# V rows gathered as 32 tokens of four experts each, multiplied by 128x32 stacks of diagonals in four column groups

## The chip, the cores and the metric

One of the cores of a Trainium2 chip runs the whole kernel. The metric is device time in microseconds, from the first to the last instruction of an execution; the median of several executions counts.

## The reference

A decoder layer on 512 tokens of width 1024: gated mixers, a cross-attention, and then a channel mixer with 16384 single-neuron experts, of which each token picks 128 (8 heads, the best 16 of each). Only the last part is touched:

```python
def chunk_fn(args):
    xb, ib, gb = args                  # 128 tokens, their expert numbers (128 each), their gates
    u = expert_u[ib]                   # (128, 128, 1024) rows of the U table
    act = jax.nn.gelu(jnp.einsum('ced,cd->ce', u, xb))
    return jnp.einsum('ce,ced->cd', gb * act, expert_v[ib])
out = lax.map(chunk_fn, (xc, ic, gc))
```

So each token needs 128 dot products with its own U rows and then the weighted sum of 128 V rows of its own. All is float32; both tables are 64 MB.

## The kernel before, in words

**Steps and slots.** The tokens are four tiles of 128. Tile and head make 32 groups of 16 steps; a step (512 in all, called tau or a slot) is one expert of each of the 128 tokens of a tile. In step n GpSimd gathers 128 rows of U, one per token (`u_rows`, eight places, L576; 512 KB), and VectorE forms the 128 dot products (`dot`, L1391). When a group of 16 is through, `gelu` on VectorE and ScalarE turns dots and gates into weights in eight parts over the next eight slots. `select` on VectorE picks the experts of a group, two pieces per slot, about two groups ahead. Steps 0 to 255 are tiles 0 and 1 (h = 0) and run under the front layers of tiles 2 and 3; steps 256 to 511 are tiles 2 and 3 (h = 1). Slots below are counted from step 256 (`HSTEPS`). Every engine walks the slots in the same order and does what lists give for each; they wait for each other only through data and places.

**V for tiles 0 and 1, densely.** From one-hot vectors of the two halves of each expert's number the kernel makes the whole matrix of weights, tokens by experts, and multiplies it with the whole V table. 64 chunks: `one_hots` on VectorE (every third of the first 32 partly on ScalarE, `first_hots`), `gate_chunk` on TensorE (L886), `take_gates` on ScalarE. 128 blocks: the SP queue brings 512 KB of V each in four places (`d_rows`), `dense_block` multiplies (L896). Chunks 0 to 31, blocks 0 to 63, chunks 32 to 63, blocks 64 to 127, by `CH_SLOT` and `BLK_SLOT`.

**V for tiles 2 and 3, by gathers.** V row m (0 to 255) is expert e = m mod 16 of group 16 + m div 16, for 128 tokens. GpSimd gathers it (L590) in `v_rows`, 6 places at first and 8 from the second chunks on, and at the end also in `u_rows`; a place is free when the pair of its last row is multiplied (`wait_used`, `v_used`). V_SLOT says at which slot row m is multiplied; the gather stands `V_AHEAD` = 4 slots later in GpSimd's order, which itself may be 8 slots ahead of the dots. A gather that waits for its place holds up all gathers behind it, U rows too. ScalarE makes a diagonal matrix of the row's 128 weights (`diagonal`, L1091): two diagonals of 64x64, one below the other, in eight places (`DRING`), two slots ahead, four slots behind in the last slots. `expert_pair(m)` on TensorE multiplies rows m and m + 1: odd rows are gathered with the token halves exchanged (`idx_turned`, made at L1384; their weights are exchanged at L1436), so that with two rows each of the four 64x64 tiles of the array has a result of its own: row half r and result half o, eight matmuls of 64x64 by 64x512 for a pair, in four banks. `add_experts(i)` on VectorE (L1468) adds both pairs of banks to tile 2 + i, the first at the slot after row 127 and the second at the end. TensorE waits for the first before row 128, as both tiles use the same banks.

**The end.** After the last rows: `add_experts(1)`, the norm of ScalarE (`finish_norm`), the scaling (`finish`, L1482), the store by the SP queue (L537).

**How a matmul shows in the trace.** A float32 matmul is two records, each with its weight load. A pair of V rows is 16 records, a dense block 8, a chunk 16.

## Time and profile before

| | us |
|---|---|
| median of 3 runs | 2024.65 (2023.76 to 2026.74) |
| span of the profiled execution | 2043.0 |
| TensorE busy | 1942.4 (95%) |
| VectorE busy | 1190.6 (58%) |
| GpSimd busy | 870.7 (43%) |
| ScalarE busy | 445.9 (22%) |
| DMA | 613.48 MB, mean 300 GB/s |

The profile is of one execution on the slowest (here the only) core, with times from its first instruction. PE is TensorE, PEld its weight loads, DVE VectorE, ACT ScalarE, POOL GpSimd, SP the sync engine; SPq is a queue of transfers. A line such as L846 is a line of the kernel. In the rows below a name such as `ps<-v_rows,diag` is result and operands, x16 a count; in a timeline, what stands in brackets is the idle time before and what ended it. "DMA share" is how busy the 16 DMA engines were together, over 1 where their packets overlap. Some matmul records can be missing from a trace.

### The profile page before, as it was taken

The page shows a single profiled execution, that of the slowest core. Times are in us where ns is not written, and L with a number is a line of the kernel's source. Part 1 is how long each engine was busy: PE and PEld are TensorE (multiplying, and loading weights), DVE is VectorE, ACT ScalarE, POOL GpSimd, SP SyncE. Part 2 cuts the span into 40 slices and gives each one's busy share as a digit, 9 for nine tenths or more (in the row PEclk, how much of TensorE's full clock was granted, in tenths as well). Part 3 has the DMA queues.
Part 4 walks back from the last instruction along what each step waited for, and adds up shares of the span by engine and source line. Part 5 has one row for each costly group of instructions (what it writes and reads, how often), then busy time and mean ns, then how long its engine had stood idle before and what let it go on. Part 6 is the DMA issues. An engine that isn't in the chain of part 4 may idle for free.

```text
span 2043.0 us, 23964 instructions
## 1 busy us (share of the span) xinstructions
PE 1942.4 (95%) x9007; PEld 1255.0 (61%) x9007; DVE 1190.6 (58%) x2972; ACT 445.9 (22%) x1045; POOL 870.7 (43%) x785
## 2 busy tenths in 40 slices
PE   8999999999889999999998888999999989999998
PEld 7688886956775887885676765444445543333332
DVE  1022101003896888788899989887867775444321
ACT  2233211111202454121211354000013321101112
POOL 0000000000684423445658355844557776666543
PEclk9999999999999999999999568999999999999999
DMA  7543454434999877999899677999999999999997
GB/s 237 147 121 109 148 155 144 145 103 136 373 388 349 280 255 239 369 386 388 331 359 371 221 261 243 410 409 409 409 376 348 344 334 410 409 409 409 409 389 278
DMA packets 252439, 613.48 MB, mean 300 GB/s; under 512 B 18676, under 2 KB 121124, under 8 KB 252324
## 3 DMA queue, kind: packets, MB, share of 16 engines
q0 software_dynamic: 110592, 402.70, 52.5%
q1 hardware_dynamic: 141120, 208.17, 29.7%
q8 instruction: 72, 1.18, 0.2%
q10 hardware_dynamic: 612, 1.07, 0.2%
q14 instruction: 43, 0.35, 0.0%
HBM read 609.77 MB, written 2.10 MB: 300 GB/s over the span
## 4 chain that ended last, share of the span: by engine, by line
PE 65%; DMA 13%; DVE 9%; POOL 7%; issue 3%; another core or an unknown queue 1%; ACT 1%; SPq 0%; POOLq 0%; DVEq 0%; ACTq 0%
PE ps L617 26%; PE ps L896 11%; PE ps L846 8%; DMA u_rows<-in_peer_u_dram,idx 7%; PE ps L632 7%; POOL u_rows L576 5%; DVE u_rows L1391 4%; PE ps L886 3%; PE ps L659 3%; POOL v_rows L590 2%; DMA wring<-in_w_in_dram 2%; DMA v_rows<-in_peer_v_dram,idx_turned 2%; PE ps L646 1%; PE ps L685 1%
## 5 line engine op out<-in xcount | busy, mean ns | idle before, releaser
L576 POOL DMA_INDIRECT u_rows<-in_peer_u_dram,idx x512 | 584.5, 1142 | 977.1 <-DVE idx L1378 508.2
L1391 DVE CUSTOM_DVE_ANT_0 u_rows<-u_rows,xn 128x1024 f32<-128x1024 f32 x512 | 621.3, 1217 | 177.8 <-DMA u_rows<-in_peer_u_dram,idx 165.2
L617 PE MATMUL ps<-xT,wring 128*128 128x256 f32 x2432 | 553.1, 386 | 22.3 <-DMA wring<-in_w_in_dram 10.1
L617 PEld LDWEIGHTS ps<-xT,wring 128*128 128x128 f32 x2432 | 464.0, 193 | 90.8 <-DMA wring<-in_w_in_dram 11.0
L896 PE MATMUL ps<-d_rows,gates 128*128 128x512 f32 x1024 | 456.3, 600 | 0.8 <-issue 0.8
L896 PEld LDWEIGHTS ps<-d_rows,gates 128*128 128x128 f32 x1024 | 190.7, 191 | 266.6 <-issue 266.6
L846 PE MATMUL ps<-v_rows,diag 64*64 64x512 f32 x1928 | 256.9, 633 | 18.9 <-DMA v_rows<-in_peer_v_dram,idx_turned 16.4
L590 POOL DMA_INDIRECT v_rows<-in_peer_v_dram,idx x121 | 135.4, 1119 | 131.3 <-PE ps L846 98.6
L886 PEld LDWEIGHTS ps<-hot_b,hot_a 128*128 128x128 f32 x1024 | 147.2, 230 | 55.4 <-issue 36.0
L886 PE MATMUL ps<-hot_b,hot_a 128*128 128x64 f32 x1024 | 155.0, 318 | 19.3 <-DVE hot_b L1458 11.0
L1091 ACT ACTIVATE diag<-ident,wgt 128x64 f32<-128x64 f32 x256 | 75.8, 336 | 435.6 <-PE ps L846 351.5
L846 PEld LDWEIGHTS ps<-v_rows,diag 64*64 64x64 f32 x1928 | 71.3, 138 | 162.1 <-issue 149.0
L590 POOL DMA_INDIRECT v_rows<-in_peer_v_dram,idx_turned x120 | 133.3, 1111 | 36.6 <-issue 34.7
L1450 DVE TENSOR_TENSOR hot_a<-e1T,iota_a 128x1024 f32<-128x1024 f32 x54 | 65.6, 1214 | 39.6 <-remote 27.1
L1123 ACT ACTIVATE gates<-ps 128x512 f32<-128x512 f32 x64 | 66.7, 1062 | 70.4 <-PE ps L886 67.5
L1231 DVE SCALAR_TENSOR_TENSOR spb_a<-ps,spb_a 128x384 f32<-128x384 f32 (+1 forms) x16 | 13.2, 824 | 85.6 <-ACT spb_a L1018 85.0
L1250 DVE TENSOR_TENSOR merged<-ps,sgc 128x256 f32<-128x256 f32 x16 | 6.7, 421 | 91.5 <-PE ps L617 91.5
L617 PE MATMUL ps<-qT,wring 128*128 128x256 f32 x256 | 56.8, 380 | 1.4 <-DMA wring<-in_w_branch_attn_dram 1.4
L617 PE MATMUL ps<-yconv,wring 128*128 128x256 f32 x256 | 56.8, 380 | 0.9 <-DMA wring<-in_w_branch_conv_dram 0.9
L632 PE MATMUL ps<-wring,xT 128*128 128x512 f32 x128 | 55.6, 592 | 0.0
L617 PEld LDWEIGHTS ps<-qT,wring 128*128 128x128 f32 x256 | 48.7, 190 | 8.3 <-DMA wring<-in_w_branch_attn_dram 1.8
L617 PEld LDWEIGHTS ps<-yconv,wring 128*128 128x128 f32 x256 | 48.7, 191 | 7.7 <-DMA wring<-in_w_branch_conv_dram 1.3
(201 smaller groups left out, 1747.0 us busy)
## 6 DMA issues: line engine op xcount, KB each, us to landing
wring<-in_w_in_dram SPq DMA_DIRECT2D x128, 512.0 KB
d_rows<-in_peer_v_dram SPq DMA_DIRECT2D x128, 512.0 KB
wring<-in_peer_w_query_dram SPq DMA_DIRECT2D x32, 512.0 KB
wring<-in_w_branch_conv_dram SPq DMA_DIRECT2D x16, 512.0 KB
wring<-in_w_branch_attn_dram SPq DMA_DIRECT2D x16, 512.0 KB
wring<-in_w_out_dram SPq DMA_DIRECT2D x16, 512.0 KB
wring<-in_xattn_wq_dram SPq DMA_DIRECT2D x16, 512.0 KB
wring<-in_xattn_wo_dram SPq DMA_DIRECT2D x16, 512.0 KB
```

The source lines that it names most:

```text
L576: pool.indirect_dma_start(out=u_rows[:, n % URING, :], out_offset=None, in_=peer_u[0], in_offset=bass.IndirectOffsetOnAxis(ap=experts_of(g ...
L590: pool.indirect_dma_start(out=v_row(m), out_offset=None, in_=peer_v[0], in_offset=bass.IndirectOffsetOnAxis(ap=own, axis=0)).then_inc((v_r ...
L617: mm = pe.matmul(bank(job)[:, 0:HN], w[:, k % 4, P * b:P * (b + 1)], act[:, k, :], start=(k == 0), stop=(k == KT - 1))
L632: mm = pe.matmul(bank(job + i), act[:, k, P * i:P * (i + 1)], w[:, k % 2, :], start=(k == 0), stop=(k == KT - 1))
L659: mm = pe.matmul(bank(job + i), act[:, k, P * i:P * (i + 1)], w[:, k % 2, :], start=(k == 0), stop=(k == KT - 1))
L846: mm = pe.matmul(ps[o:o + 64, 2 * (r // 64) + c, :], diag[r:r + 64, k % DRING, :], v_row(k)[r:r + 64, BANK * c:BANK * (c + 1)], start=firs ...
L886: mm = pe.matmul(ps[:, 4 + ch % 4, 64 * t:64 * (t + 1)], hot_a[:, 8 * (ch % 2) + t, :], hot_b[:, ch % 2, t, :], start=True, stop=True)
L896: mm = pe.matmul(ps[:, 4 + 2 * i + c, :], gates[:, j % 64, P * i:P * (i + 1)], d_rows[:, j % 4, BANK * c:BANK * (c + 1)], start=(j % 64 == ...
L1091: act.activation(diag[:, m % DRING, :], ident64[:, :], ACT.Copy, scale=wgt[:, g, e:e + 1]).then_inc(diag_rdy, 1)
L1123: act.activation(gates[:, :, t:t + 8].rearrange("p b t -> p t b"), ps[:, 4 + ch % 4, :].rearrange("p (t b) -> p t b", t=8), ACT.Copy).then ...
L1391: dve.tensor_tensor_reduce(out=u, in0=u, in1=(xn2 if h else xn1)[:, i, :], scale=1.0, scalar=0.0, op0=ALU.mult, op1=ALU.add, accum_out=dot ...
L1450: dve.tensor_tensor(hot_a[:, 8 * (ch % 2):8 * (ch % 2) + 8, :], e1T[:, i, o:o + 8].unsqueeze(2).to_broadcast([P, 8, P]), iota_a[:, :].unsq ...
```

## The change

Row m = 16 g + 4 s + b now holds, for token block b of 32 tokens, four experts: partition 32 q + j is the V row of token 32 b + j for its expert 4 q + s. With a stack of four 32x32 diagonals as the stationary (128x32) one matmul sums over the four experts and gives 32 tokens. Rows m to m + 3 (b = 0 to 3) make up the 128 tokens, in the four column groups of the array.

- `expert_quad(m)` for `expert_pair(m)`: 8 matmuls of 128x32 by 128x512 for four rows, in place of 8 of 64x64 by 64x512 for two. Each token tile has two banks of its own, so `add_experts` is one addition per tile and the wait for `hadd` goes. Places of V rows are freed by fours.
- Indices and weights must be laid out by blocks: 16 small copies per group on VectorE (`idx_quad`, in the last four pieces of `select`) for two, and 16 small copies per group on ScalarE (`spread_weights`) for the exchange in the last part of `gelu`, which is one product now. `gelu` waits in part 4 until the last group's weights are spread.
- `diag` is 128x32 in 12 places for 128x64 in 8. A diagonal is made no earlier than its group's weights (`WEIGHTS_AT`).
- `v_rows` has 6 places, 8 from the slot where GpSimd is past the selection of tile 2, 10 past that of tile 3.
- The lists of slots are new. Chunks begin at slot 16 for 12, blocks at 52 for 48 and at 181 for 179. V rows by slot:

| slots | rows before | slots | rows after |
|---|---|---|---|
| 24 to 46 | 22 | 24 to 46 | 26 |
| 48 to 150 | 14 | 46 to 80 | 25 |
| | | 115 to 150 | 7 |
| 151 to 177 | 84 | 150 to 178 | 104 |
| 179 to 256 | 110 | 178 to 210, 210 to 240, 240 to 256 | 32, 31, 9 |
| 256 to 280 | 26 | 256 to 268, 268 to 280 | 17, 5 |

```diff
-    URING, VRING, DRING, GRING, IRING = 8, 8, 8, 4, 8
+    URING, VRING, DRING, GRING, IRING = 8, 10, 12, 4, 8
+    BLOCK = P // 4
...
-    CH_SLOT = spread(12, 46, 32) + spread(151, 177, 32)
+    CH_SLOT = spread(16, 46, 32) + spread(151, 177, 32)
...
-    BLK_SLOT = spread(48, 149, 64) + spread(179, 260, 64)
-    V_SLOT = (spread(24, 46, 22) + spread(48, 150, 14) + spread(151, 177, 84) + spread(179, 256, 110)
-              + spread(256, 280, 26))
+    BLK_SLOT = spread(52, 149, 64) + spread(181, 260, 64)
+    V_SLOT = (spread(24, 46, 26) + spread(46, 80, 25) + spread(115, 150, 7) + spread(150, 178, 104) + spread(178, 210, 32) + spread(210, 240, 31) + spread(240, 256, 9) + spread(256, 268, 17) + spread(268, 280, 5))
...
+    WEIGHTS_AT = [HSTEPS + TOPK * (g + 1) + 8 for g in range(HG)]
     for m, slot in enumerate(V_SLOT):
         V_OF.setdefault(slot + V_AHEAD, []).append(m)
-        DIAG_OF.setdefault(slot + (DIAG_BEHIND if slot >= STEPS - 16 else -DIAG_AHEAD), []).append(m)
-        if m % 2:
-            PAIR_OF.setdefault(slot, []).append(m - 1)
+        DIAG_OF.setdefault(max(slot + (DIAG_BEHIND if slot >= STEPS - 16 else -DIAG_AHEAD), WEIGHTS_AT[m // TOPK]),
+                           []).append(m)
+        if m % 4 == 3:
+            QUAD_OF.setdefault(slot, []).append(m - 3)
...
-    V_LATE = next(m for m in range(HSTEPS) if V_SLOT[m] >= CH_SLOT[32])
+    V_GROWS = {next(m for m in range(HSTEPS) if V_SLOT[m] + V_AHEAD > TOPK * (HG + PH * (n + 1) - 1)): n
+               for n in range(HT)}
...
         def wait_used(eng, m):
-            eng.wait_ge(v_used, m // 2 + 1)
+            eng.wait_ge(v_used, m // 4 + 1)
...
-                        pool.wait_ge(turned, 2 * (g + 1))
-                    own = idx_turned[:, g, e // 2:e // 2 + 1] if e % 2 else idx2[:, g, e:e + 1]
+                        pool.wait_ge(quad_idx, 16 * (g + 1))
                     pool.indirect_dma_start(
                         out=v_row(m), out_offset=None, in_=peer_v[0],
-                        in_offset=bass.IndirectOffsetOnAxis(ap=own, axis=0)
+                        in_offset=bass.IndirectOffsetOnAxis(ap=idx_quad[:, g, e:e + 1], axis=0)
                     ).then_inc((v_ready if kind == "v" else u_ready)[place], 16)
...
-            def expert_pair(m):
+            def expert_quad(m):
                 if m == 0:
                     pe.wait_ge(wt_done, 2 * SBH)
-                if m == HSTEPS // 2:
-                    pe.wait_ge(hadd, 2)
-                pe.wait_ge(diag_rdy, m + 2)
-                for k in (m, m + 1):
-                    wait_row(pe, k)
-                first, last = m % (HSTEPS // 2) == 0, m % (HSTEPS // 2) == HSTEPS // 2 - 2
+                tile, n = m // (HSTEPS // 2), m % (HSTEPS // 2)
+                pe.wait_ge(diag_rdy, m + 4)
+                for b in range(4):
+                    wait_row(pe, m + b)
                 for c in range(2):
-                    for k, turn in ((m, 0), (m + 1, 64)):
-                        for r in (0, 64):
-                            o = (r + turn) % P
-                            mm = pe.matmul(ps[o:o + 64, 2 * (r // 64) + c, :], diag[r:r + 64, k % DRING, :],
-                                           v_row(k)[r:r + 64, BANK * c:BANK * (c + 1)],
-                                           start=first, stop=last)
+                    for b in range(4):
+                        mm = pe.matmul(ps[BLOCK * b:BLOCK * (b + 1), 2 * tile + c, :], diag[:, (m + b) % DRING, :],
+                                       v_row(m + b)[:, BANK * c:BANK * (c + 1)],
+                                       start=(n == 0), stop=(n == HSTEPS // 2 - 4))
                 mm.then_inc(v_used, 1)
...
+            def spread_weights(g):
+                act.wait_ge(wgt_rdy, HG + g + 1)
+                for b in range(4):
+                    for q in range(4):
+                        to = wgt[BLOCK * q:BLOCK * (q + 1), g, :].rearrange("p (s b) -> p s b", b=4)[:, :, b]
+                        qw = act.activation(to, gl[BLOCK * b:BLOCK * (b + 1), 3, 4 * q:4 * (q + 1)], ACT.Copy)
+                qw.then_inc(quad_wgt, 1)
...
-                    act.wait_ge(v_used, (m - DRING) // 2 + 1)
-                act.activation(diag[:, m % DRING, :], ident64[:, :], ACT.Copy,
+                    act.wait_ge(v_used, (m - DRING) // 4 + 1)
+                act.activation(diag[:, m % DRING, :], ident32[:, :], ACT.Copy,
                                scale=wgt[:, g, e:e + 1]).then_inc(diag_rdy, 1)
...
+                if tau in WEIGHTS_AT:
+                    spread_weights(WEIGHTS_AT.index(tau))
...
-                    odd = idx2[:, g - HG, :].rearrange("p (e two) -> p e two", two=2)[:, :, 1]
-                    for r in (0, 64):
-                        dve.tensor_copy(idx_turned[64 - r:P - r, g - HG, :], odd[r:r + 64, :]).then_inc(turned, 1)
+                    for b in range(4):
+                        for q in range(4):
+                            to = idx_quad[BLOCK * q:BLOCK * (q + 1), g - HG, :].rearrange("p (s b) -> p s b", b=4)
+                            dve.tensor_copy(to[:, :, b], idx2[BLOCK * b:BLOCK * (b + 1), g - HG,
+                                                              4 * q:4 * (q + 1)]).then_inc(quad_idx, 1)
+                        yield
...
                     dve.wait_ge(gate_rdy, g + 1)
+                    if g > HG:
+                        dve.wait_ge(quad_wgt, g - HG)
...
-                for r in range(2):
-                    if r:
-                        dve.wait_ge(hadd, 2 * i + 1)
-                    dve.tensor_tensor(hh, ps[:, 2 * r:2 * r + 2, :].rearrange("p c n -> p (c n)"), hh,
-                                      ALU.add).then_inc(hadd, 1)
+                dve.tensor_tensor(hh, ps[:, 2 * i:2 * i + 2, :].rearrange("p c n -> p (c n)"), hh,
+                                  ALU.add).then_inc(hadd, 1)
```

## Rows read from the trace of the kernel before

**Rows 1.** The page's slices: GB/s of the transfers, 40 slices of 51 us

```profile
GB/s 237 147 121 109 148 155 144 145 103 136 373 388 349 280 255 239 369 386 388 331 359 371 221 261 243 410 409 409 409 376 348 344 334 410 409 409 409 409 389 278
```

**Rows 2.** Windows, all engines: stretch, length, busy time of each, clock, DMA share, GB/s

```profile
1130.00:1268.00 138.00, 120.81 (x689) 95.50 (x690) 128.35 (x272) 70.39 (x151) 63.57 (x59) 0.67 0.71 231
1268.00:1505.00 237.00, 234.32 (x624) 100.25 (x623) 185.99 (x531) 9.44 (x42) 135.54 (x124) 1.00 1.02 405
1505.00:1678.00 173.00, 156.56 (x1201) 87.50 (x1202) 137.36 (x269) 53.12 (x123) 127.09 (x109) 0.96 0.95 343
1678.00:1972.00 294.00, 293.68 (x1236) 107.82 (x1240) 117.66 (x303) 32.13 (x114) 183.29 (x174) 1.00 1.02 407
1972.00:2043.00 71.00, 60.93 (x352) 21.87 (x344) 11.89 (x20) 12.71 (x41) 26.57 (x28) 0.97 0.80 300
```

**Rows 3.** Timeline of TensorE, pieces of E, D and B: start, length, instructions

```profile
1835.65 3.70 PE L896 MATMUL ps<-d_rows,gates 128*128 128x512 f32 x8
1839.29 3.66 PE L846 MATMUL ps<-v_rows,diag 64*64 64x512 f32 x32
1842.88 7.13 PE L896 MATMUL ps<-d_rows,gates 128*128 128x512 f32 x16
...
1518.49 2.00 PE L886 MATMUL ps<-hot_b,hot_a 128*128 128x64 f32 x16
...
1203.55 3.68 PE L886 MATMUL ps<-hot_b,hot_a 128*128 128x64 f32 x16 [1.48 <-DVE hot_b L1458]
1207.16 3.69 PE L846 MATMUL ps<-v_rows,diag 64*64 64x512 f32 x16
```

**Rows 4.** Timeline of TensorE, the column groups of L711 in the first half

```profile
116.32 0.43 PE L711 MATMUL ps<-wbuf_a,vbuf 128*64 128x256 f32 x1
116.33 0.43 PE L711 MATMUL ps<-wbuf_b,vbuf 128*64 128x256 f32 x1
116.59 0.38 PE L711 MATMUL ps<-wbuf_a,vbuf 128*64 128x256 f32 x1
```

**Rows 5.** Groups of instructions by shape, VectorE, stretch B

```profile
L1450 DVE TENSOR_TENSOR hot_a<-e1T,iota_a 128x1024 f32<-128x1024 f32 x22 | 26.6, 1209 | 6.0 <-PE ps L886 4.8 <-issue 1.1
...
L1384 DVE COPY idx_turned<-idx 64x8 uint32<-64x8 uint32 x4 | 0.7, 165 | 0.1
```

**Rows 6.** Timeline, small work of ScalarE and VectorE in B

```profile
1166.24 0.20 ACT L1081 ACTIVATE gl<-gl 128x16 f32<-128x16 f32 x1
...
1174.61 0.35 ACT L1091 ACTIVATE diag<-ident,wgt 128x64 f32<-128x64 f32 x1 [4.26 <-DVE wgt L1436]
...
1173.88 0.70 DVE L1436 SCALAR_TENSOR_TENSOR wgt<-gl,gate_r 128x8 f32<-128x8 f32 x3
```

**Rows 7.** Waits, stretch E: engine and line, waited for, us, times, longest

```profile
DVE u_rows L1391 <- DMA u_rows<-in_peer_u_dram,idx: 121.9, 51, 5.2
...
DVE hbuf L1468 <- issue: 21.0, 1, 21.0
```

**Rows 8.** Timeline of VectorE at the end

```profile
2034.30 2.48 DVE L1468 TENSOR_TENSOR hbuf<-ps,hbuf 128x1024 f32<-128x1024 f32 x2 [8.51 <-PE ps L846]
```

**Rows 9.** Windows of L896 and of L846 alone, stretch F

```profile
1972.00:2043.00 71.00, 28.97 (x64) 11.77 (x64) 0.97 0.80 300
...
1972.00:2043.00 71.00, 32.74 (x288) 10.11 (x280) 0.97 0.80 300
```

**Rows 10.** Chain of work that ended last, one piece in C: start, length, what

```profile
1363.42 17.13 DMA u_rows<-in_peer_u_dram,idx
```

**Rows 11.** Timeline, a gather of D and the pair that uses its row

```profile
1573.71 1.02 POOL L590 DMA_INDIRECT v_rows<-in_peer_v_dram,idx_turned  x1 [0.30 <-issue]
...
1579.93 1.52 PE L846 MATMUL ps<-v_rows,diag 64*64 64x512 f32 x12 [0.47 <-DMA v_rows<-in_peer_v_dram,idx_turned]
```

**Rows 12.** Timeline of GpSimd, stretch F

```profile
1997.45 0.94 POOL L590 DMA_INDIRECT v_rows<-in_peer_v_dram,idx  x1 [0.30 <-issue]
```

**Rows 13.** Waits, stretch F

```profile
POOL v_rows L590 <- PE ps L846: 16.8, 5, 4.2
```

42 lines of the change are left out of this document (21 added, 21 removed).

## The prediction

> **What bounds the kernel now.** I read the page's shares of engines first, then its slices, then the same figures cut at the borders of the work. TensorE is busy 95% of the span, but from slice 24 on slices with 409 GB/s stand beside slices with a quarter to a half less [rows 1]. Both are near a limit, so the question is which of them ends last in each stage. The change touches only what comes after 1130 us, so I cut that part in five [rows 2]:
>
> - B, 1130 to 1268: one-hot chunks 0 to 31, 22 V rows. VectorE busy 128.35 of 138 us, 231 GB/s, TensorE's mean clock 0.67.
> - C, 1268 to 1505: dense blocks 0 to 63, 14 V rows. TensorE 234 of 237 us, 405 GB/s: both full.
> - D, 1505 to 1678: chunks 32 to 63, 84 V rows. TensorE 157 and GpSimd 127 of 173 us, 343 GB/s.
> - E, 1678 to 1972: dense blocks and V rows. TensorE 293.68 of 294 us, 407 GB/s: both full again.
> - F, 1972 to 2043, the end: 300 GB/s.
>
> The most that any slice shows is 409 GB/s, at a DMA share of 1.03. A gather or a block of the V table is 512 KB, so a transfer costs 524288 / 409000 = 1.28 us when the queues are full. No byte is removed by this change: 256 V rows are gathered before and after. A stage can only win what it leaves of 409 GB/s: B 138 x (1 - 231/409) = 60 us, C 2, D 28, E 1, F 19. That is 110 us, and it is the ceiling of any gain here. In E DMA is as full as TensorE, so halving TensorE's work gives nothing unless V rows move out of E, and where they go they cost at least their transfer.
>
> **Part 1, the multiplication.** A pair of V rows is 8 matmuls of a 64x64 stationary, 16 records; in E two pairs take 3.59 us from start to start, 1.80 each [rows 3]. Afterwards four rows are 8 matmuls of 128x32, again 16 records of 512 columns. If four column groups run side by side as the four 64x64 tiles do, a quad also costs 1.80: 64 quads are 115 us in place of 128 pairs, 230. No row shows four groups. The nearest is L711: two 128x64 column groups, each with its own moving tile, start at 116.32 and 116.33, and the next two begin 0.26 later [rows 4]. So two groups take the time of one, with weights of all 128 rows loaded under running matmuls. Bounds for a quad: 1.80 (all four), 3.6 (two at a time), and 16 x 0.455 = 7.3 us (none; 0.455 is a record of L896, 8 in 3.64 us from start to start [rows 3]). I take 1.80, because the nearest row has full overlap. Below 1.80 nothing speaks for: the records stream as many columns.
>
> [...]
>
> **Part 2, the new small work.** VectorE: 16 index copies per group of 16 steps in place of 2, and one weight product in place of three. Copies stand at 165 ns [rows 5] and three products take 0.70 us [rows 6]. 14 x 0.17 - 0.45 = +1.9 us per group. In C and E VectorE waits for U rows (122 us in E [rows 7]) and hides it; in B it is the bound. Four groups (16 to 19) are selected before B ends, so +7.6 us there. ScalarE: 16 tiny copies per group. The shortest ScalarE row is 0.20 us [rows 6]; a diagonal of 64 columns takes 0.35 at most places and is the high bound [rows 6]. So 3.2 to 5.6 us per group, I take 3.5. ScalarE is busy 70 of 138 us in B and 53 of 173 in D [rows 2] and has room, but everything behind it on its queue (the diagonals, the takings of gates) is late by as much once per group. PE waits for that where a quad needs fresh weights; in B that is group 17 at slot 40. It is cheap: 2 us. GpSimd's two additions for the identity come once before B; nothing. One add of experts in place of two: 2.48 us for two [rows 8], so -1.2 us at the end. The first token tile's add also moves on VectorE, from slot 184 to 169, into the chunks of D; it now waits 21 us for TensorE in E [rows 7], where dots are behind it and U rows cover it. In D one-hots are behind it, but TensorE is within a chunk or two of VectorE there, so at most two chunks of 2.00 us and a quad, 6 us; I leave it in D's 9 us of waits, of which TensorE's own share goes away. TensorE's wait for hadd at row 128 goes (the second tile has banks of its own); TensorE is never idle there, so nothing. The wait for quad_wgt ahead of the product in gelu: behind it on VectorE is the next dot. ScalarE passes spread_weights 8 slots after a group's end, the wait comes 20 slots after it. Nothing, while ScalarE is under 12 slots late.
>
> **Part 3, the places.** V rows by stage, from the lists of slots: B 22 to 26, C 14 to 32, D 84 to 104, E and F 136 to 94. A quad can't start before its group's weights, which are ready 8 slots after the group's last dot. From group 10 on the lists put the first quad of a group 2 to 6 slots before that, so TensorE must lag VectorE by about 5 slots in E. Now it lags similarly: 8 blocks (64 records) and 36 V rows (288) are left to it when the dots are through [rows 9].
>
> *B.* It ends at slot 46, not 48: -4 us (two slots of 1.2 us of dot and 0.7 of selection). +7.6 VectorE, +2 ScalarE. 6 quads for 11 pairs, and VectorE's 6 us of idling ahead of its one-hots shrink [rows 5]: -4. Sum about +1; bounds -6 and +10.
>
> *C.* 237 us x 405 GB/s is 183 transfers; +18 V and +2 U of the two slots are 203, x 1.28 = 260 us. TensorE needs 64 x 3.64 + 8 x 1.80 = 247 and is no longer the bound. +23; low bound +12 (TensorE's 247 and 2). High bound: V has six places here, so of a quad's four rows two are issued only after the quad before. Three gathers, a landing as long as the 17 us of a U row [rows 10] and 2 us of quad are 23 us, and slots 46 to 80 want a quad every 16.7 (5.4 slots of 2.4 transfers). Over 6 quads that would be 38 us, but fewer transfers in flight land sooner; a fifth of it stays: +30.
>
> *D.* GpSimd issues every gather: 109 in 127.09 us, 1.17 each, plus 0.30 between two [rows 2, 11], so 1.47 a gather. 28 U + 84 V = 112 x 1.47 = 164, and 9 us of waits make the 173 of now. Afterwards 132 x 1.47 = 194 + 9 = 203. TensorE's 27 x 1.80 + 63 = 112 us are far below. +30. Low end 132 x 1.28 = 169 plus 9 = 178 (+5), if GpSimd's durations fall to the 0.94 that it shows where VectorE is quiet [rows 12]; high end in rival 1.
>
> *E and F.* 294 x 407 + 71 x 300 GB/s are 269 transfers; 42 fewer are 227, x 1.28 = 291 us. TensorE: 64 x 3.64 + 23.5 x 1.80 = 275, below. Behind the last byte come the last quad (2 us) and then add, norm, scaling and store: 9 us from the adds on now, to the span's end at 2043.0 [rows 8]; -1.2, so 10 in all. 301 for 365: -64, of which 54 are the 42 rows and 10 the end, where GpSimd now waits for TensorE (16.8 us in five waits [rows 13]) and the queues stand empty. Bounds -70 and -50.
>
> **Sum.** +1 +23 +30 -64 = -10 us of the profiled span of 2043.0. The three timed runs have a median of 2024.65, 18 us less than the span, so I carry the difference over: 2014.6, -0.5%.
>
> **Rivals.**
>
> 1. *Places freed by quads, and the clock, starve D: slower.* A place is freed only when all four rows are used. From a quad's end, four V rows and a U are issued (4.08 x 1.47 = 6.0 us to the last), it lands 6.2 later (issued 1573.71, used 1579.93 [rows 11]), the quad takes 1.9: 14.1 us for two quads, 7.05 each, under GpSimd's 5.08 x 1.47 = 7.5. But TensorE has work for 112 of 203 us. It was busy 157 of 173 at clock 0.96 now, and 121 of 138 at 0.67 in B [rows 2]; there, at half clock, 16 records take 3.69 us in place of 1.80 and a chunk 3.68 in place of 2.00 [rows 3]. At half clock D needs 27 x 3.69 + 32 x 3.68 = 217 us, so D is bound by it, and the cycle of places becomes (14.1 + 1.8 + half a chunk) / 2 = 8.9 x 26 = 231. D between 217 and 231, +44 to +58, for +30: the sum is +4 to +18, say 2036. It decides once the clock stays at half for more than 203/217 of D. For it: the clock of B. Against it: B's 0.67 is no half (0.50) either; TensorE that has fallen behind is busy and gets its clock back, and in D it would be busy at half clock.
> 2. *Column groups only by twos.* Quad 3.6 us: C 233 + 29 = 262, +25; D 27 x 3.6 + 63 = 160, under its bound, +30; E 233 + 85 + 9 = 327, -38. The sum with B is +18: 2042. None at all: C +54, D 27 x 7.3 + 63 + 9 = 269, +96, E 233 + 172 + 9 = 414, +49: 2225.
> 3. *GpSimd speeds up and D and B gain more.* D +5, B -4, C and E at their middle: -40, 1985. For it: GpSimd's gathers are 1.17 in D and 0.94 in F [rows 12]. Against it: VectorE, beside which they are long, has the same work in D.
> 4. *It is hidden.* The four terms cancel to within 4 us: what E loses is what C and D take, 42 rows at 1.28 there against 38 at 1.28 to 1.47 here. Time 2021 to 2028.
>
> [...]
>
> **How the numbers follow.** Forecast (-4 to -25 us) 0.42; rival 3 (beyond -25) 0.16; rival 4 0.17; rival 1 0.18; rival 2 0.07. A change of 0.2%, 4 us, is about what a measurement of this kernel tells from none. Faster 0.58, same 0.17, slower 0.25. The range takes in rival 3 to its middle, rival 1 whole and rival 2's first case: 1988 to 2043. The likeliest case alone is 2000 to 2021.
>
> **What would show it.** Part 1: a stretch of two quads takes 3.6 us, the matmuls of the four column groups start together, and all of them 115 us busy. C: 405 to 409 GB/s with TensorE idle for 10 us or more, waiting for V rows. D: 200 us or so, GpSimd back to back, TensorE near 60% busy, its clock the thing to look at. E: 300 us to the end, no longer 100% TensorE, VectorE's wait for U rows shorter. End: 409 GB/s to within 20 us of the last byte. I am wrong if a quad takes over 2 us at full clock, if D takes over 215 us, or if the queues are not full in C and E, for then TensorE waits for V rows whose places are not free and blocks and dots wait behind it.

## The result and the profile after

Measured: 2055.91 us, median of 4 runs (2052.8 to 2058.24), against 2025.7 (2023.76 to 2027.34) for the kernel before beside them. The ratio is 1.0139 [1.0116, 1.0162]: slower by 1.4%, 41 us above the forecast of 2014.6 and 13 above the upper end of its range, 2043.

The windows of the changed kernel. Their borders are events, since the lists of slots moved: first one-hot chunk, first dense block, end of the 64th block, the next block, end. I call the five stretches A to E; A is what lies ahead of the prediction's B (here from 1000 us), and E takes in its F. Columns as in [rows 2].

```profile
1000.00:1135.94 135.94, 113.00 (x474) 79.70 (x472) 129.84 (x372) 16.88 (x45) 92.83 (x75) 0.93 0.98 356
1135.94:1288.17 152.23, 122.99 (x640) 99.25 (x640) 138.87 (x319) 79.73 (x201) 81.02 (x70) 0.60 0.69 238
1288.17:1528.40 240.23, 236.08 (x612) 100.40 (x608) 180.41 (x559) 30.51 (x145) 150.36 (x126) 0.98 1.02 405
1528.40:1750.36 221.96, 158.77 (x945) 88.13 (x945) 147.45 (x301) 65.66 (x190) 152.68 (x137) 0.72 0.93 335
1750.36:2051.00 300.64, 273.51 (x884) 107.70 (x880) 129.09 (x345) 44.13 (x191) 166.57 (x155) 0.96 0.99 388
```

Cut by the same events, the profiled execution of before is A 133.1, B 134.7, C 234.5, D 175.5, E 365.2 us. So E is 64.6 us shorter, as forecast, and A to C are 26 longer where 24 were forecast; D is 222 us for 175.5, +46.5 where +30 was forecast. Its clock fell from 0.96 [rows 2] to 0.72. D lies in the 31st to 34th slices, which have 316 to 340 GB/s; before, it had 334 to 348 in the 31st to 33rd [rows 1].

```profile
PEclk9999999999999999999998565999996877999999
...
GB/s 236 151 116 114 147 150 148 139 113 135 382 386 391 275 246 256 384 389 389 329 361 353 215 232 262 386 402 409 409 398 316 337 340 339 393 395 384 407 409 339
```

The quad (four V rows multiplied together) is itself what was hoped for. TensorE in D (start, length, instructions): 16 records of 128x32 in 1.92 us at full clock (granted 1.00 from 1583.40 to 1588.40) and in 3.64 at half clock (0.50 from 1548.40 to 1558.40), and ahead of most quads of D a wait for a V row.

```profile
1558.31 3.64 PE L849 MATMUL ps<-v_rows,diag 128*32 128x512 f32 x16
...
1575.64 3.64 PE L849 MATMUL ps<-v_rows,diag 128*32 128x512 f32 x16 [3.52 <-DMA v_rows<-in_peer_v_dram,idx_quad]
1579.21 4.19 PE L889 MATMUL ps<-hot_b,hot_a 128*128 128x64 f32 x32
1583.33 1.92 PE L849 MATMUL ps<-v_rows,diag 128*32 128x512 f32 x16
1585.19 2.00 PE L889 MATMUL ps<-hot_b,hot_a 128*128 128x64 f32 x16
1589.55 2.94 PE L849 MATMUL ps<-v_rows,diag 128*32 128x512 f32 x16 [2.37 <-DMA v_rows<-in_peer_v_dram,idx_quad]
```

The waits of D, changed kernel (engine and line, what for: us, times, longest):

```profile
DVE hot_a L1463 <- PE ps L889: 60.6, 15, 9.3
PE ps L849 <- DMA v_rows<-in_peer_v_dram,idx_quad: 50.5, 20, 6.8
POOL v_rows L597 <- PE ps L849: 34.4, 13, 14.5
...
POOL v_rows L597 <- issue: 29.2, 91, 1.7
...
PE ps L849 <- ACT diag L1102: 10.2, 1, 10.2
```

TensorE waits for V rows, GpSimd can't issue them because TensorE hasn't given their places back, and VectorE's one-hots and U gathers queue behind both. That is a ring of waits with no engine full: TensorE 159, GpSimd 153, VectorE 147 of 222 us. GpSimd is the nearest to full: with the 0.30 us between two of its 137 gathers it is taken for 194. In D of the kernel before it waited 13.8 us for TensorE (and 8.1 more for something that its trace doesn't name), TensorE 16.4 for V rows.

### The profile page after: what moved, and what is told of

Its sections match the earlier page's. It is cut to its first block, busy times and chain, and to the rows that moved or that the text cites. A ratio compares the mean times of both kernels' runs of the same rounds, so it can differ in the third digit from the quotient of the medians.

```text
span 2051.0 us, 22378 instructions
## 1 busy us (share of the span) xinstructions
PE 1865.9 (91%) x7983; PEld 1234.3 (60%) x7983; DVE 1221.0 (60%) x3162; ACT 488.5 (24%) x1301; POOL 898.6 (44%) x787
## 3 DMA queue, kind: packets, MB, share of 16 engines
q1 hardware_dynamic: 141120, 208.17, 29.6%
## 4 chain that ended last, share of the span: by engine, by line
PE 55%; DMA 16%; POOL 11%; DVE 10%; issue 6%; ACT 2%; POOLq 0%; ACTq 0%; DVEq 0%
PE ps L624 25%; PE ps L899 8%; DMA u_rows<-in_peer_u_dram,idx 7%; PE ps L639 7%; POOL v_rows L597 6%; DVE u_rows L1407 5%; POOL u_rows L584 5%; DMA v_rows<-in_peer_v_dram,idx_quad 5%; PE ps L849 5%; PE ps L889 3%; PE ps L666 2%; DMA wring<-in_w_branch_attn_dram 2%; DMA wring<-in_w_in_dram 1%; PE ps L653 1%; PE ps L692 1%
## 5 line engine op out<-in xcount | busy, mean ns | idle before, releaser
L584 POOL DMA_INDIRECT u_rows<-in_peer_u_dram,idx x512 | 607.5, 1186 | 907.7 <-DVE idx L1391 507.9
L597 POOL DMA_INDIRECT v_rows<-in_peer_v_dram,idx_quad x247 | 276.8, 1121 | 223.2 <-PE ps L849 143.3
L849 PE MATMUL ps<-v_rows,diag 128*32 128x512 f32 x988 | 171.3, 818 | 101.7 <-DMA v_rows<-in_peer_v_dram,idx_quad 69.8
L889 PEld LDWEIGHTS ps<-hot_b,hot_a 128*128 128x128 f32 x1024 | 165.7, 256 | 71.6 <-DVE hot_b L1471 38.7
L889 PE MATMUL ps<-hot_b,hot_a 128*128 128x64 f32 x1024 | 172.5, 344 | 26.4 <-DVE hot_b L1471 24.4
L849 PEld LDWEIGHTS ps<-v_rows,diag 128*32 128x32 f32 x988 | 34.2, 133 | 188.1 <-issue 144.6
L1102 ACT ACTIVATE diag<-ident,wgt 128x32 f32<-128x32 f32 x256 | 62.2, 307 | 157.5 <-PE ps L849 157.1
L1091 ACT ACTIVATE wgt<-gl 32x4 f32<-32x4 f32 x256 | 52.9, 207 | 139.2 <-DVE gl L1451 136.4
```

What stands on the lines that cost most here:

```text
L584: pool.indirect_dma_start(out=u_rows[:, n % URING, :], out_offset=None, in_=peer_u[0], in_offset=bass.IndirectOffsetOnAxis(ap=experts_of(g ...
L597: pool.indirect_dma_start(out=v_row(m), out_offset=None, in_=peer_v[0], in_offset=bass.IndirectOffsetOnAxis(ap=idx_quad[:, g, e:e + 1], ax ...
L849: mm = pe.matmul(ps[BLOCK * b:BLOCK * (b + 1), 2 * tile + c, :], diag[:, (m + b) % DRING, :], v_row(m + b)[:, BANK * c:BANK * (c + 1)], st ...
L889: mm = pe.matmul(ps[:, 4 + ch % 4, 64 * t:64 * (t + 1)], hot_a[:, 8 * (ch % 2) + t, :], hot_b[:, ch % 2, t, :], start=True, stop=True)
L1091: qw = act.activation(to, gl[BLOCK * b:BLOCK * (b + 1), 3, 4 * q:4 * (q + 1)], ACT.Copy)
L1102: act.activation(diag[:, m % DRING, :], ident32[:, :], ACT.Copy, scale=wgt[:, g, e:e + 1]).then_inc(diag_rdy, 1)
```

## The experiments

All ratios below are to the kernel before on the same chip. Even so they compare only within one of two kinds of chips: on two chips (e1 to e8) the kernel before had a median of 2042 us and the changed one a ratio of 1.0076 (e7); on the others (e9 to e18) it had 2026 to 2027, as in the result above with its 1.0139. The changed kernel itself takes the same time on both, 2055.7 and 2055.9 us; the kernel before does not. e2 to e6 and e8 were run on the first kind alone, and the runs that mend the loss (e10, e12, e14, e15, e17, e18) on the second alone, so a step from one group to the other mixes the edit with the kind of chip. To compare stretches I use "left": a stretch's length x (1 - its GB/s / 409), my estimate of the time by which its bytes could have been moved sooner; 409 to 411 GB/s is the most that a slice of any of these profiles shows. Each figure for a stretch is of one profiled execution.

**e1_before, e16_before: the kernel before, one profile each.**

> The kernel before, profiled once more. The profile that the prediction rests on has a span of 2043.0 us beside timed runs of 2024 to 2027; the profiled run of the changed kernel (2051.0) lies 5 us under its own median. If the 18 us were an effect of profiling on this kernel, this span is again near 2043 with the same stages (B 135, C 237, D 173, E with the end 365). If that execution was merely a slow one, this span is 2022 to 2030, and the missing 15 to 20 us stand in one or two places of the stages, which then were mis-sized in the sum.

> The kernel before, unchanged, one profile. Both of its profiles so far leave 27 and 28 us of 409 GB/s in D; e10, e13 and e14 leave 16, e15 leaves 27. If D's loss belongs to the kernel, it is 26 to 28 us again; if it differs from execution to execution, it may be 16 as in e13, which in D has the same form and the same eight places.

2034.93 us on a chip of the first kind (D 174.7 us, 26.9 left), and 2024.75 on one of the second. The latter, windows as above:

```profile
1126.86:1257.38 130.52, 116.89 (x689) 92.06 (x689) 123.31 (x259) 70.41 (x151) 60.72 (x57) 0.69 0.71 233
1257.38:1493.10 235.72, 234.66 (x628) 100.38 (x624) 184.44 (x532) 9.44 (x42) 140.98 (x125) 1.00 1.02 404
1493.10:1659.28 166.18, 146.56 (x1200) 84.53 (x1201) 140.20 (x271) 53.24 (x122) 123.50 (x109) 0.97 0.98 366
1659.28:2022.90 363.62, 354.36 (x1588) 129.57 (x1584) 129.50 (x322) 44.98 (x155) 213.41 (x202) 0.99 0.98 387
```

D takes 166.2 us and leaves 17.5, where the execution on which I built the sum took 175.5 and left 27.9. So what D leaves differs by 10 us between profiles of one kernel. Whether executions or chips differ so isn't settled: e1 is of the first kind and e16 of the second, and the chip of the profile of [rows 2] isn't on record. The execution of [rows 2] was 20 us longer than this one: 9.2 in A to C (6.2 of them in A, which the change hardly touches), 9.3 in D, 1.6 in E. Against e16, the changed kernel costs +35 in A to C, +56 in D and -63 in E.

**e2_quads_old_lists: the changed kernel with the lists of slots of before.**

```
-    CH_SLOT = spread(16, 46, 32) + spread(151, 177, 32)
-    BLK_SLOT = spread(52, 149, 64) + spread(181, 260, 64)
+    CH_SLOT = spread(12, 46, 32) + spread(151, 177, 32)
+    BLK_SLOT = spread(48, 149, 64) + spread(179, 260, 64)
(and V_SLOT)
```

> The changed kernel (quads, stacks of diagonals, 12 diagonals, the new small work) with the three lists of slots of the kernel before. Theory A, the places: the loss comes from moving 42 V rows forward into stages where places are freed by fours and TensorE falls to half clock. Then B takes 5 us more than before for the small work, C as before, D 168 to 178 us (21 quads at 8.0 us, the rate that the changed kernel shows), E with the end 345 to 357: 2010 to 2030. Theory B, the quads themselves: the small work of VectorE and ScalarE and the waits for whole quads cost wherever they stand. Then D is 185 or more, B 150, and the time 2040 to 2060.

1.0043 [1.0015, 1.0071]. Slower without the new lists too: D leaves 36.9 us, for 26.9 in e1 on the same chip. TensorE waits 47.1 us there for V rows (5.5 in e1), GpSimd 29.6 for TensorE (17.0). The end gained: the last 66 us leave 11.8 for 19.8.

**e3_pairs_new_lists: pairs of 64x64 with the new lists.**

```
-            PAIR_OF.setdefault(slot, []).append(m - 1)
+            PAIR_OF.setdefault(V_SLOT[m | 3], []).append(m - 1)
```

> The kernel before (pairs of 64x64) with the new lists of slots; both pairs of four rows stand at the slot of the last row, and a diagonal is made no earlier than its group's weights, as the new lists need. Eight places at the most. Theory A: D is bound by places and a low clock; pairs keep TensorE busier (54 pairs are 97 us for 49) and free places a little sooner, so D is 195 to 210 for 217, E TensorE-bound at 327 to 340 for 301; 2055 to 2080. Theory B: without the quads' small work B falls back to 137 and D to 190, and the whole is below 2045.

1.0121 [1.0054, 1.0188]. Both pairs of four rows stand at the slot of the fourth. The end leaves 26.5 us: pairs can't keep up there. D leaves most of all, 48.7, although a pair frees its places by itself. It holds two things together, the new lists and pairs put off to the fourth row's slot; no run has pairs at their own slots with the new lists.

**e4_filler: the changed kernel with two unused matmuls per one-hot chunk, ahead of the wait for it.**

```
+                for _ in range(2):
+                    pe.matmul(ps[:, 4 + ch % 4, :], ident[:, :], xn2[:, 0, 0:BANK], start=True, stop=True)
                 pe.wait_ge(hot_rdy, ch + 1)
```

> The changed kernel with two matmuls of 128x128 by 128x512 (four records, 1.8 us at full clock) ahead of each chunk's wait for its one-hots, in the chunk's own bank, which the chunk then overwrites. If the half clock is what costs in B and D, the mean clock rises to 0.9 or more, a chunk takes 2.0 and a quad 1.9 us for 3.6, and D falls from 217 to about 200, B by 5 us: 2030 to 2040. If places and landings bound D whatever the clock, the clock rises and D stays at 210 to 220, and the time is 2050 to 2065; if the filler itself gets in the way, TensorE has 58 us more in each of B and D and the time rises over 2065.

1.0076 [1.0044, 1.0107], the same as the changed kernel on the other chip of that kind (e7). Its window of D:

```profile
1528.60:1755.59 226.99, 185.09 (x1073) 99.06 (x1073) 148.52 (x306) 66.18 (x190) 149.21 (x137) 0.88 0.91 328
```

The granted clock rose from 0.72 to 0.88 in D and from 0.60 to 0.92 in B (151.6 us), and neither got shorter. The unused matmuls take time themselves (TensorE is busy 185 us in D for 159, 135 in B for 123), so this run alone doesn't say that the clock is free. e6 and e17 say more: they have the same halves, clocks of 0.91 and 0.95 in D, and D takes 219.7 us in one and 195.2 in the other.

**e5_pairs_by_fours: the kernel before, only that who waits for a free place waits for four rows at a time.**

```
-            eng.wait_ge(v_used, m // 2 + 1)
+            eng.wait_ge(v_used, 2 * (m // 4) + 2)
```

> The kernel before with one edit: a place of a V row is free only when all four rows of its four are multiplied (the pairs, the lists and the rest stay). Theory A, places freed by fours cost: in D GpSimd waits longer for TensorE, TensorE longer for V rows, and what D leaves of 409 GB/s rises from 27 us to 33 to 38, the whole is 5 to 12 us slower than before, nearly all of the +7 us that quads with the old lists show in D. Theory B, it is the quad's own matmuls or waits: the same time as before to within 3 us.

1.0031 [1.0009, 1.0053]. D leaves 36.5 us where e1 leaves 26.9, and GpSimd waits 28.9 us for TensorE where it waited 17.0. So releasing by fours costs 0.3% by itself, without a quad. That D then leaves what it leaves in e2 rests on one profile of each, and e16 shows that such a figure can differ by 10 us in one kernel.

**e6_halves: the changed kernel, rows 0 to 159 multiplied and freed by twos, both halves at the quad's slot.**

```
+                for part in ((0, 1), (2, 3)) if m < HALVED else ((0, 1, 2, 3),):
+                  pe.wait_ge(diag_rdy, m + part[-1] + 1)
```

> The changed kernel, but rows 0 to 159 are multiplied and freed by twos (two column groups at a time, TensorE waits for two rows, not four); from row 160 on quads as they are. Theory A, places: D's transfers leave 30 to 34 us of 409 GB/s in place of 40, D falls from 222 to 212 to 216, B by 0 to 5, TensorE's mean clock in D rises over 0.85 as its work there doubles: 6 to 15 us under the changed kernel. Theory B, D is bound by GpSimd's issuing and by the late weights alone: no change, within 4 us of the changed kernel. It also tells the price of two column groups: 3.6 us for four rows if only two run at a time.

1.0074 [1.0044, 1.0103] for e7's 1.0076: nothing, where theory A wanted 6 to 15 us. D's clock was 0.91 and its length 219.7, and GpSimd waited 30.0 us for TensorE in it, TensorE 32.2 for V rows. The first half is still asked for only when the fourth row is due, so by my estimate its places come back about the length of a half ahead of the second's (1.91 us for 8 records, at 1600.80).

**e7_after: the changed kernel again, on e6's chip.**

> The changed kernel again, beside the kernel before on this chip, as the partner for the others of this call: 1.2 to 1.6% slower than before, with the stages that it showed (B 152, C 240, D 222, E 301).

1.0076 [1.0049, 1.0103], where 1.012 to 1.016 were expected; D 229.5 us, 44.9 left, clock 0.69.

**e8_indices_by_act: e2 with the 16 index copies on ScalarE.**

```
-                            dve.tensor_copy(to[:, :, b], idx2[BLOCK * b:BLOCK * (b + 1), g - HG,
-                                                              4 * q:4 * (q + 1)]).then_inc(quad_idx, 1)
+                        act.activation(to[:, :, b], idx2[BLOCK * b:BLOCK * (b + 1), g - HG, 4 * q:4 * (q + 1)],
+                                       ACT.Copy).then_inc(quad_idx, 1)
```

> Quads with the old lists, and the 16 small copies of indices per group on ScalarE, not on VectorE. If VectorE's new small work is what B (and the stretch before it, where the last front layers end) pay, both fall back by 2 us per group made there, 6 to 8 us in all, and the time is that of the kernel before or up to 4 us below: the end's gain of 7 to 10 pays for D. If ScalarE's copies (3.5 us a group, and 7 now) are what holds up diagonals and the takings of gates, it is 3 to 8 us slower than quads with the old lists.

1.0022 [0.9999, 1.0045], 0.2% under e2; the intervals overlap. A to C are 505.6 us for 501.5, so one profile doesn't show the gain where it was expected, and D is unchanged (37.6 left).

**e9_quads_after_weights: the changed kernel, each quad not before its weights are due.**

```
-            QUAD_OF.setdefault(slot, []).append(m - 3)
+            QUAD_OF.setdefault(max(slot, WEIGHTS_AT[m // TOPK] + 2), []).append(m - 3)
```

> The changed kernel, only that a quad is put at the later of its own slot and two slots after its group's weights are due (WEIGHTS_AT + 2), so that from group 10 on TensorE takes dense blocks where it now stands before a diagonal that isn't ready. Gathers and all other places are as they were. In the changed kernel TensorE waits for diagonals 10.2 us in D and 27.6 us in E, D's stretch from the last chunk to block 64 is 24 us for 7 in the kernel before, and D and E leave 10 to 20 us of 409 GB/s outside the chunks. Theory A (late weights: the stalls hold up the places of V rows and so the gathers): the waits fall under 5 us, the stretch after the last chunk falls to about 10 us, the whole is 4 to 8 us under the changed kernel, ratio to before 1.003 to 1.005. Theory B (the stalls are covered, since in E the transfers and not TensorE end last): the waits go and the time stays within 2 us of the changed kernel's, ratio about 1.0075.

1.028 [1.0252, 1.0308], 26 us above the changed kernel: a clear miss of both theories. The waits for diagonals went as said, but these came in E (changed kernel: 71.0 for GpSimd, none of TensorE for `v_rows`):

```profile
POOL v_rows L597 <- PE ps L849: 103.8, 11, 22.6
...
PE ps L849 <- DMA v_rows<-in_peer_v_dram,idx_quad: 51.8, 6, 12.5
```

A quad put later holds four places for longer. D is 16 us shorter (206.4) and E 38 longer (338.3). TensorE gained nothing by not standing still, and the gathers stood instead: 360 GB/s in E for 388.

**e10_mixed, e18_mixed_again: old lists, e8's index copies, and rows 0 to 119 multiplied and freed by twos, each half at its own slot; quads from row 120 on.**

```
+        def used_by(m):
+            return m // 2 + 1 if m < HALVED else HALVED // 2 + (m - HALVED) // 4 + 1
...
-                pe.wait_ge(diag_rdy, m + 4)
-                for b in range(4):
+                bs = (m % 4, m % 4 + 1) if m < HALVED else range(4)
...
+                for b in bs:
```

> The lists of slots of the kernel before, quads with the 16 index copies on ScalarE (as e8), but V rows 0 to 119 (all of B, C and D) are multiplied and freed two at a time, each half of a quad at its own slot of the old lists, and whole quads only from row 120 on. Theory A (freeing four places at once is what costs D 10 us, and the quad's gain comes at the end of the program): D leaves about 27 us of 409 GB/s, as the kernel before, for 37 in e8; the last 66 us leave 12 to 15 for 19 in the kernel before; ratio 0.996 to 0.999. Theory B (D is slow for another reason that all quad forms share, such as a diagonal that needs all 128 rows of both V rows and the weights spread late): D still leaves 36 us or so and the ratio stays 1.001 to 1.003.

> e10 again, unchanged, on another chip and beside the two kernels above. Ratio 0.992 to 0.996 again; D leaves 15 to 17 us of 409 GB/s if that belongs to the kernel, or up to 27 if it differs between executions.

0.994 [0.9918, 0.9962], and on another chip 0.9949 [0.9928, 0.9969]: 2016.1 and 2015.8 us, faster than both kernels, and more than theory A had asked for. D leaves 15.8 and 15.5 us, no more than e16's 17.5; the price of the fours is gone. (e8, the same without the halving, has 1.0022, but on the other kind of chip.) The last 66 us leave 12.3 and 10.2 for e16's 17.6. e18's D and E:

```profile
1490.20:1652.29 162.09, 143.92 (x848) 80.09 (x848) 133.05 (x250) 59.78 (x161) 122.38 (x110) 0.93 0.98 370
1652.29:2008.20 355.91, 303.85 (x1056) 113.55 (x1056) 128.48 (x315) 72.39 (x324) 213.76 (x202) 0.94 1.00 397
```

**e11_first_places_old: the changed kernel with chunks from slot 12, dense blocks from 48, and V rows as 22 in slots 24 to 46 and 36 in 48 to 150.**

```
-    V_SLOT = (spread(24, 46, 26) + spread(46, 80, 25) + spread(115, 150, 7) + ...
+    V_SLOT = (spread(24, 46, 22) + spread(48, 150, 36) + ...
```

> The changed kernel, with the first places nearer to the old lists: one-hot chunks from slot 12, dense blocks from 48, V rows 22 in slots 24 to 46 and 36 in slots 48 to 150 (for 26, 25 and 7). From slot 150 on all is as in the changed kernel. Theory A (B is 17 to 22 us longer than before because the first dense block, four slots later, stands behind V rows that have not landed, and V rows are crowded in at slots 46 to 80): B falls from 150 to about 137 us and C rises from 240 to 245 to 250 us, so A, B and C together lose 5 to 10 us and the ratio is 1.003 to 1.005. Theory B (what B gives back C takes, since both must move the same bytes): A + B + C stay within 3 us of the changed kernel's 527, ratio about 1.0075.

1.0097 [1.007, 1.0124], 8 us under the changed kernel, though not as theory A had it: B fell to 138.6, but C rose to 263.0, and A to C were 536.0 for 528.4. The gain lay in D (214.8 for 222.0), and D of the changed kernel differs by as much between its two profiles. The intervals of the two ratios overlap a little (1.0124 and 1.0116), so that the first places cost something is likely; by what path isn't shown.

**e12_new_lists_mixed: e10 with the new lists, halves down to row 159. e17_new_lists_mixed_dve: the same with the index copies back on VectorE, that is, the changed kernel with the halving alone.**

```
-            QUAD_OF.setdefault(slot, []).append(m - (1 if m < HALVED else 3))
+            QUAD_OF.setdefault(max(slot, WEIGHTS_AT[m // TOPK]) if m < HALVED else slot, []).append(m - (1 if m < HALVED else 3))
```

> The changed kernel's lists of slots with the form of e10: V rows 0 to 159 multiplied and freed two at a time, each half of a quad at its own slot (not before its group's weights), whole quads from row 160 on; index copies on ScalarE. Theory A (the changed kernel is slow because four places are held until a quad's last row has landed; its lists are sound): D leaves about 20 us of 409 GB/s for 40 to 45 in the changed kernel, the whole is near e10's, ratio 0.990 to 0.998. Theory B (the lists themselves cost 8 to 10 us: late weights, V rows ahead of the first dense block, more gathers in D than GpSimd and the queues carry): the ratio is 1.001 to 1.007, that is 8 us or more above e10.

> The changed kernel with the halving alone: its lists, its 16 index copies on VectorE, rows 0 to 159 multiplied and freed by twos, each half at its own slot. It differs from e12 only by the engine of the index copies, and from e6 only in that the first half doesn't wait for the quad's slot. Theory A (places and landings held by fours are what made the change slow): ratio 1.001 to 1.004, that is 12 us or more under the changed kernel, and 2 to 6 us above e12 for VectorE's copies. Theory B (the halving needs VectorE's copies out of B to be worth anything): ratio 1.006 or more.

e12: 0.999 [0.9976, 1.0005]. e17: 1.0021 [1.0003, 1.0038]. The halving alone takes the changed kernel from 1.0139 to 1.0021, some 24 us; moving the index copies to ScalarE seems to take off 0.3% more (the intervals just touch). e17's windows of B to E, and its waits in D:

```profile
1135.92:1285.02 149.10, 122.61 (x640) 88.29 (x641) 140.17 (x324) 81.46 (x209) 81.63 (x70) 0.73 0.71 242
1285.02:1532.50 247.48, 247.48 (x622) 101.52 (x624) 178.44 (x554) 29.54 (x139) 140.40 (x129) 1.00 1.02 407
1532.50:1727.69 195.19, 156.29 (x936) 82.32 (x936) 147.66 (x301) 69.70 (x188) 148.73 (x134) 0.95 0.97 364
1727.69:2028.40 300.71, 270.91 (x884) 106.41 (x880) 129.21 (x345) 44.13 (x191) 167.73 (x155) 0.96 0.98 388
```

```profile
PE ps L856 <- DMA v_rows<-in_peer_v_dram,idx_quad: 21.4, 18, 3.3
...
PE ps L856 <- ACT diag L1109: 17.3, 9, 12.3
...
POOL v_rows L601 <- PE ps L856: 11.2, 14, 5.5
```

The stretches A and E are those of the changed kernel to 0.1 us. D is 27 us shorter, of which GpSimd's wait for places gives 23 (34.4 to 11.2); C is 7 longer, B 3 shorter. TensorE's busy time in D is the same, 156 for 159 us: a half takes 1.91 us for two rows, twice the time per row, and the clock is 0.95. So it isn't the amount of TensorE's work that made D long.

```profile
1588.30 1.91 PE L856 MATMUL ps<-v_rows,diag 128*32 128x512 f32 x8 [0.33 <-DMA v_rows<-in_peer_v_dram,idx_quad]
1590.86 1.91 PE L856 MATMUL ps<-v_rows,diag 128*32 128x512 f32 x8 [0.65 <-ACT diag L1109]
```

As kernels, e6 and e17 differ only in the slot of the first half. e6 gained nothing on the changed kernel of its kind of chip, e17 1.2%. So what matters seems to be when the first rows are used, not only how their release is counted, and e3 fits it. The two never ran on the same kind of chip: the kernel before, which also frees by twos, is itself 0.8% faster on e17's kind, where the changed kernel is not, so how much e17's edit would gain on e6's kind isn't known.

The lists alone, all else as in e10 but for the rows that are halved (160 for 120): 0.999 against 0.994, so they cost about 0.5%, 8 us by the medians; e12 thus fell between the ranges of its two theories. In e12 A to C are 525.2 us for e18's 490.2, D 194.8 for 162.1, E 299.9 for 355.9: what moves out of E comes back with 12 us on top. (e18's profile is of its fastest execution; against e10's, of its slowest, the same sum is -2 us, so the medians decide.)

**e13_pairs_ten_places: the kernel before with V's places of the changed one.**

```
-        if m == V_LATE:
-            ring = [("v", n, None) for n in (6, 7)] + ring
+        if m in V_GROWS:
+            ring = [("v", 6 + 2 * V_GROWS[m] + n, None) for n in range(2)] + ring
```

> The kernel before, with nothing changed but V's places: places 6 and 7 from the row at slot 108 on (in place of slot 151) and two more, 8 and 9, from slot 236 on, as in the changed kernel. Pairs of 64x64, old lists, 8 diagonals. Theory A (e10's gain over before comes from places): D leaves about 16 us of 409 GB/s for 26, the ratio is 0.994 to 0.997. Theory B (places don't matter in D, where both have eight; e10's gain comes from its narrower diagonals and their twelve buffers): D stays at 25 us, the last 66 us leave 15 us or less for 19, ratio 0.997 to 1.000.

0.9998 [0.9985, 1.001]. D left 15.9 us, which looked like theory A until e16 showed 17.5 for the kernel before itself. The places alone are worth nothing.

**e14_all_by_twos: e10, all 256 rows by twos. e15_mixed_8_diagonals: e10, DRING 8 in place of 12.**

```
-    HALVED = 120
+    HALVED = 256
(e15:)
-    URING, VRING, DRING, GRING, IRING = 8, 10, 12, 4, 8
+    URING, VRING, DRING, GRING, IRING = 8, 10, 8, 4, 8
```

> e10, but all 256 rows are multiplied and freed two at a time, so the quad form's one advantage, half of TensorE's time per V row, is gone everywhere. Theory A (in E DMA is as full as TensorE, so halving TensorE's work there gives only the last 5 to 8 us): E + end 368 us for 362.6, ratio 0.997 to 0.999. Theory B (quads at the end give nothing, or cost by holding places, and TensorE's lag is covered): the time is within 2 us of e10's, ratio about 0.994.

> e10 with eight buffers for diagonals (DRING) in place of twelve. ScalarE waits for TensorE before diagonals 59.8 us of 140 in D in the kernel before (8 buffers) and 15.9 in e10 (12), and gates stand behind them on its queue. Theory A (the four further buffers free ScalarE's queue and with it the chunks, which is where D's 10 us come from): D leaves 25 us of 409 GB/s, the time is about 8 us above e10's, ratio 0.998. Theory B (ScalarE's waits are covered): within 2 us of e10's, ratio about 0.994.

e14: 0.997 [0.9951, 0.9989]; e15: 0.9945 [0.9926, 0.9965], on one chip. The diagonals' buffers do nothing for the time. Yet D leaves 26.5 us in e15's profile, for 15.8 and 15.5 in e10 and e18: 10 us of what D leaves in one profile say nothing about a kernel's median, and the D figures of e1, e2 and e5 must be read with that in mind. The quads at the end are worth about 0.25%, some 5 us; the intervals overlap, so it is likely and not settled (E is 360.4 us in e14, 362.6 and 355.9 in e10 and e18). e14 is already 0.3% faster than the kernel before. What it has in common with e10, and e13 lacks, is the smaller work of VectorE (no copies of indices, one weight product, one add of experts for two; busy 680 us from 1000 us on, for 696 in e13), but also the 128x32 diagonals and their buffers. That VectorE's work is the cause is not shown.

## Why the prediction was wrong, step by step

- *The quad, 1.80 us: right.* 16 records take 1.92 us (1.86 from start to start, 2000.74 to 2002.60), all four column groups side by side. Every load of a quad uses all 128 rows; the loads' mean is 133 ns, they run under the matmuls (eight of them from 2000.74 on, beside the first records), and no time is added between quads: four in a row, 64 records, take 7.07 us (2032.32 to 2039.39). Rival 2 is out.
- *A to C, +24: right in sum* (+26), not in parts: B and A +20 for +1, C +6 for +23, so the hit is in part luck. A part of the difference is the border: I let B end two slots earlier, at the last chunk, but the first dense block went from slot 48 to 52. The wait that I had not seen is one of 10.89 us for V rows, ahead of the last quad before the first dense block. Against e16 it is +35; between e12 and e17 the copies of indices make 7 (525.2 and 532.5), forecast as 7.6, though A to C of the kernel before alone spread from 491.0 (e1) to 502.3 us.
- *D, +30: wrong, the step that failed.* The sum was 132 gathers x 1.47 = 194 and the 9 us of waits of the kernel before carried over (with the 109 gathers that its trace has in D, for the 112 of the lists, they would have been 13). The 194 was fair (137 gathers at 1.12 + 0.30 us are 194 too). The waits were the term that failed: what is left of D's 222 us is 28, and GpSimd's waits for places are 34.4 in the view above. In rival 1 I had the cycle of places, 7.05 us a quad at full clock, and put it aside because GpSimd's 7.5 was larger. Its landing of 6.2 us was right (5.0 to 7.6, median 6.1, in D), and yet a quad of D takes 222 / 26 = 8.5 us. That two cycles of nearly one length, which also wait for TensorE's chunks in between, cost more than the larger of the two is my reading; no run varies them one by one. With places freed by twos and each half at its own slot (e17) the same lists give D 195.2 us, and e12 194.8, where 203 was forecast. So the sum for D holds, with 8 us to spare, for a kernel that uses and frees by twos, and this one doesn't. (As a difference it is +20 to the profile that the sum started from and +29 to e16's.)
- *E and the end, -64: right.* -64.6. TensorE is no longer full there (273.5 of 300.6 us), and the queues nearly are: 388 GB/s at a DMA share of 0.99.
- *The 18 us carried over: wrong.* The sum gave a span of 2033; the changed kernel's was 2051.0, 18 above. The other 23 us of the miss are here: I took 18 off for the distance from the profiled execution to the median, as if it belonged to the kernel. The changed kernel's median lies 5 us above its profiled span. e16 shows that the profiled execution was a long one, in A, B and D. It may have been one on a chip of the first kind: none of the 61 timed executions of the kernel before on the second kind took more than 2035.3 us, and the median of the first kind is 2042. The record doesn't say which chip it was, so this stays open; either way the span and the median were not of like executions.
- *Rival 1* named the mechanism (places, 0.18) and gave D +44 to +58, which was met with +46.5, but by the wrong half of its argument: it wanted TensorE at half clock as the bound, for more than 203/217 of D. Of D's 222 pieces of 1 us, 107 show 0.50, 84 show 1.00 and 31 something between, so with the mean of 0.72 D was at half clock for some 55%; TensorE was busy 159 of 222 us. The point against it, that a busy TensorE gets its clock back, held late in one place: TensorE was busy without a gap from 1540.54 to 1564.4, and the clock was 0.50 until 1562. e4 raised the clock and gained nothing, at the price of its own matmuls; e6 had 0.91 and gained nothing; e5 kept 0.94 and was slower than the kernel before by 0.3%. Rival 3 is out: a V gather takes 1.12 us on average in the changed kernel. Rival 4 counted bytes alone.
- *Late weights from group 10 on*: TensorE does wait for them, 10.2 us in D and 17.4 in E, and e12 waits as long (14.6 and 16.3) with a ratio of 0.999. So they don't make the 1.4%, and moving the quads out of their way (e9) cost 26 us. They can be a part of the 0.5% that the new lists cost: e10 and e18 wait 2.7 and 1.9 us in D.

Why fours cost so much with eight places is argued from e5, e6, e17 and the waits, not measured as one cycle: it may be that a quad ties up half of the places until its last row has landed and TensorE has come to its slot, so gathers for only one further quad can be under way.

Open: which path e11's 8 us take, whether the quads at the end are worth 5 us or nothing, how e6 and e17 compare on one kind of chip, and why the kernel before is 0.8% slower on the first kind and the changed one isn't.

## What to carry to other kernels

Where a ring of buffers feeds an engine, changing how many are consumed at once changes the ring too: here releasing by fours cost 0.3% with nothing else changed (e5), and using and releasing by fours 1.2% (e17), even though a row's multiplication took half the time (four rows in 1.92 us, where two took 1.95). Use the coarse form only where the consumer is the bound, and the fine form where transfers or their issue are (e10). When a forecast sets a cycle aside because another is a little longer, as 7.05 us here for 7.5, give the case in which both count its own price. And take a second profile before carrying an offset between span and median into a sum, and before reading 10 us of one stretch as the kernel's.

## What the runs showed of the hardware

- Four 128x32 column groups in float32 run side by side: 16 records of 512 columns in 1.92 us at full clock, for 1.95 with four 64x64 tiles in the kernel before (at 1571.30 us), with weights of 32 columns loaded in 133 ns on average under them. Two of the four groups alone take 1.91 us for 8 records, so leaving two groups empty saved nothing here (e17, at 1588.30).
- A V gather landed later where the queues moved more: a median of 14.2 us from issue to landing in C of the changed kernel (405 GB/s), 6.1 in D (335).
- Small work added up by its count: 48 index copies of 32x4 took 8.5 us on VectorE in B, 177 ns each, and 16 copies of weights take 3.3 us on ScalarE at 207 ns each.
- With unused matmuls ahead of TensorE's waits (e4) the granted clock was higher (0.92 for 0.60 in B, 0.88 for 0.72 in D), with TensorE busy 12 and 26 us longer there; the kernel's time stayed the same (1.0076 with and without).
- One kernel can take 0.8% longer on one chip than on another (2042 and 2026 us, the kernel before), while another form of it takes the same on both (2055.7 and 2055.9 us, the changed kernel).
